# Three unrolled loops rolled up, a TensorE wait moved to the end of its loop, and one prefetch moved behind a loop turn

## The reference

```
for i in range(DEPTH):                       # 4
    mod_x = silu_c @ w_mod[i] + b_mod[i]     # the same for the context
    hx = rms_norm(x, norm_g[i]) * (1 + scale_x) + shift_x
    oc, ox = (_rwkv7_mixer, _na_mixer, _s5_mixer)[i % 3](hc, hx, ...)
    x = x + gate_x * ox
# _rwkv7_step, for 16 heads of 64 channels, in both directions over the tokens:
    sa = einsum(state, kk)
    state = state * w - sa * (kk * a) + v * k
    y = einsum(state, r)
```

## Time and profile before

| | |
|---|---|
| time, median of 3 runs | 6884.97 us (6882.52 to 6889.81) |
| the profiled execution | 6884.97 us, its span 6883.1 us |
| PE busy | 5779.3 us (84%) |
| DVE, ACT, POOL busy | 44%, 29%, 27% |
| granted TensorE clock, mean | 0.920 |
| recurrence of layer 0, from the first window on | 808.8 to 2066 us |
| recurrence of layer 3 | 5461.6 to 6719 us |
| the S5 loop of four turns | 3859 to 4168 us |

### The profile page before, as it was taken

The page is one execution under the profiler, slowest core; times in us unless marked ns, Lnnn a source line. Parts: engine busy times, 40 slices in busy tenths (PEclk is TensorE's granted clock), DMA queues, the critical chain, the costliest instruction groups (busy, mean ns, idle before and its releaser), DMA issues. The chain is left out here.

```text
span 6883.1 us, 212951 instructions
## 1 busy us (share of the span) xinstructions
PE 5779.3 (84%) x91944; PEld 3883.9 (56%) x91944; DVE 3053.5 (44%) x6329; ACT 1984.0 (29%) x3317; POOL 1860.7 (27%) x2006
## 2 busy tenths in 40 slices
PE   5999788888888699978896984396999888888887
PEld 4555577777774355445553553343455577777773
DVE  6200366656661233145514478422300266666662
ACT  1000254444440222134302232111000244544440
POOL 4452244434340336000003540000000144444431
PEclk8999899999998899989898997698999999999998
DMA  3222100110002222132122337422111100011002
GB/s 121 86 99 81 42 30 30 43 37 30 30 30 93 111 98 80 39 95 54 49 82 103 96 94 73 124 70 97 55 69 69 49 30 30 30 43 37 30 30 89
DMA packets 196079, 443.13 MB, mean 64 GB/s; under 512 B 24768, under 2 KB 108608, under 8 KB 195648
## 3 DMA queue, kind: packets, MB, share of 16 engines
q1 hardware_dynamic: 160896, 338.58, 16.4%
q10 hardware_dynamic: 34752, 98.61, 3.6%
HBM read 329.14 MB, written 107.97 MB: 64 GB/s over the span
## 5 line engine op out<-in xcount | busy, mean ns | idle before, releaser
L357 PE MATMUL ps<-arena 128*128 128x512 f32 (+1 forms) x4672 | 1711.0, 528 | 84.9 <-DMA arena<-s_w_in 34.8
L357 PEld LDWEIGHTS ps<-arena 128*128 128x128 f32 x4672 | 886.6, 190 | 903.9 <-issue 864.7
L1861 PE MATMUL ps<-arena 64*64 64x64 f32 x35840 | 736.6, 225 | 161.4 <-ACT arena L2246 59.1
L153 POOL TENSOR_TENSOR arena<-arena 128x512 f32<-128x512 f32 (+1 forms) x360 | 329.0, 930 | 1801.9 <-DMA arena<-w_mod 1791.6
L1861 PEld LDWEIGHTS ps<-arena 64*64 64x64 f32 x35840 | 641.6, 137 | 247.7 <-issue 230.3
L2246 ACT COPY arena<-ps 128x512 f32<-128x512 f32 (+1 forms) x880 | 535.8, 630 | 535.1 <-PE ps L1861 523.1
L2389 POOL TENSOR_TENSOR arena<-arena 128x256 f32<-128x256 f32 (+1 forms) x320 | 299.6, 944 | 895.5 <-DVE arena L2610 456.5
L571 PE MATMUL ps<-arena 128*128 128x512 f32 (+1 forms) x1152 | 423.9, 528 | 41.0 <-DMA arena<-na_w_in 41.0
L1622 DVE SCALAR_TENSOR_TENSOR arena<-arena 128x1280 f32<-128x1280 f32 (+2 forms) x128 | 152.5, 1265 | 617.3 <-PE ps L357 502.7
L2314 POOL MEMSET arena<- 128x1280 f32 (+4 forms) x22 | 15.1, 739 | 1467.9 <-POOLq L83 1467.9
L156 POOL TENSOR_TENSOR arena<-arena 128x256 f32<-128x256 f32 (+2 forms) x504 | 383.1, 772 | 52.0 <-issue 2.1
(11 more groups left out here) (260 smaller groups left out, 9788.6 us busy)
## 6 DMA issues: line engine op xcount, KB each, us to landing
arena<-proj SPq DMA_DIRECT2D x158, 640.0 KB, 5.0
proj<-arena ACTq DMA_DIRECT2D x96, 640.0 KB, 3.9
arena<-w_mod SPq DMA_DIRECT2D x96, 512.0 KB, 7.6
arena<-rw_w SPq DMA_DIRECT2D x68, 512.0 KB, 3.6
arena<-xres SPq DMA_DIRECT2D x40, 640.0 KB, 6.7
xres<-arena ACTq DMA_DIRECT2D x24, 640.0 KB, 6.5
arena<-na_w_in SPq DMA_DIRECT2D x24, 512.0 KB, 3.6
arena<-x SPq DMA_DIRECT2D x16, 640.0 KB, 6.6
```

Of the source, the lines that this page charges most:

```text
L153: self.nc.gpsimd.tensor_tensor(out, strip[:, c:c + n, :], self.k.cond[:, c:c + n, s:s + 1].to_broadcast([P, n, P]), ALU.mult)
L357: last = nc.tensor.matmul(k.ps[:, 3 * u + n, 0:b - a], w[:, c * P:(c + 1) * P], src[:, c, a:b], start=(c == 0), stop=(c == KT - 1))
L1861: last = PE.matmul(part_of(out, dst, hh, g, d), part(l, src, hh, g, d), rhs, start=True, stop=True)
```

## The change

- `NORM_FILL` goes from 19 and 148 to 21 and 147.
- In `s5_prepare`, SP issues the modulation part i+4 after turn i and no more ahead of it. Part 7 stays ahead of turn 3, so the order is turn 0, part 4, turn 1, part 5, turn 2, part 6, part 7, turn 3. PE's program is as before.
- In `rwkv_recur`, PE's two waits and the hold go from the head of the turn to its end, after the last `widened`; they ask for the same events, and the credits of `scale_ev` and `y_ev` go down by 3 and 1 to fit.
- The eight turns of ACT, POOL and DVE become `Fori` loops.

```
-NORM_FILL = {0: 19, 3: 148}
+NORM_FILL = {0: 21, 3: 147}
...
                     if u % 4 == 3 and not last:
                         sp.wait_ge(chunk_mm, i * 6 + (3 + u // 4 * 3))
                         strip(i * 2 + (KT + 2 + u // 4), u // 4)
+                if not last:
+                    hidden.sync_part(sp, i + 4)
 
             with sp.Fori(0, 3) as i:
-                hidden.sync_part(sp, i + 4)
                 turn(i, False)
             hidden.sync_part(sp, 7)
             turn(3, True)
...
-            sem("gate_sig"), sem("gated", 1), sem("scale_ev", 3), sem("post_done"))
+            sem("gate_sig"), sem("gated", 1), sem("scale_ev"), sem("post_done"))
-        y_mm, y_ev = sem("y_mm"), sem("y_ev", 2)
+        y_mm, y_ev = sem("y_mm"), sem("y_ev", 1)
...
             with pe.Fori(0, KT) as e:
-                pe.wait_ge(scale_ev, e * 3 + 3)
-                pe.wait_ge(y_ev, e * (NCH // 4) + 1)
-                hold(k, pe)
                 with pe.Fori(0, NW2) as w:
                     window(e * NW2 + w, e * (NW2 + 1) + w)
...
                 def y_seen(i):
-                    return y_ev, e * (NCH // 4) + (i + 3)
+                    return y_ev, e * (NCH // 4) + (i + 2)
...
                 pe.wait_ge(bonus_ev, e * 3 + 3)
                 widened(SCALE_BANK, 2, wide_post, scale_mm)
+                pe.wait_ge(scale_ev, e * 3 + 3)
+                pe.wait_ge(*y_seen(3))
+                hold(k, pe)
...
-                act.wait_ge(y_ev, e * (NCH // 4) + 2)
+                act.wait_ge(y_ev, e * (NCH // 4) + 1)
...
-            for e in range(KT):
+            with act.Fori(0, KT) as e:
...
-            for e in range(KT):
+            with pool.Fori(0, KT) as e:
...
-            for e in range(KT):
+            with dve.Fori(0, KT) as e:
```

## The result

The changed kernel takes 7007.25 us (median of 4 runs, 7000.49 to 7023.34) against 6887.39 us (median of 4, 6882.52 to 6899.74) of the kernel before: a ratio of 1.0171, 95% interval 1.0154 to 1.0187, or 118 us on 6887 (106 to 129). Forecast were 7048 us, 163 us more, with 7012 as the low end. The sign and the places are as forecast: three new stalls in the S5 loop and a longer gap at each seam of the recurrence. What failed is the sum, above all the term for what comes back in the S5 loop, where 30 us came back for the 10 that I had taken.

What follows compares the result with a forecast made beforehand. PE's program was taken to bound the kernel, so only PE's waits move the end. From the profiled 6885 us: + 120 (S5 loop, net) + 36 (moved wait) + 3 (loops) + 4 (register work) = 7048 us, range 7012 to 7098.

Steps and rivals of the forecast that it cites:

- The direction and the places: Whole kernel slower (0.97); three new S5 waits of 43 to 44 us, about 8 us idle at 14 recurrence seams.
- The stalls: S5 loop, ends of turns 0, 1 and 2: PE waits for POOL's part, 44 + 2 x 43 = 130 us.
- The load leg: S5 loop: loads go out near 3935.5, so POOL begins the part at 3945.5; PE wants it at 3935.89.
- What comes back: S5 loop: 6 us of PE's input waits and 8 us of its DVE waits go, against 4 us clock loss.
- The clock: S5 loop, after each of three pauses: 4.7 us of work at half speed, 4 us added in all.
- The moved wait: Recurrence seams: PE's branch now follows the wait; net 2.6 us, 14 times, 36 us, bounds 14 to 59.
- the code that comes late: Recurrence, behind the seam's branch: second code block may come late; +0.5 us a seam together with a longer low clock.
- The three loops: Recurrence loops of DVE, ACT and POOL: any DVE start fetch is covered by PE's lateness; 0.2 us a seam, 3 us.
- a rival in which DVE becomes the bound: Recurrence seam: DVE's loop misses each turn, +49 us and more in place of 3, about 7094 us; chance 0.08.
- Register work: Recurrence turns: register work for the waits, at places behind a drain; 0.25 us a turn, 16 turns, 4 us.
- The windows' code no longer fits: Recurrence window loop: 64 inner branches must fetch, 3.25 us each, 208 us, or 104 in one layer; chance 0.07.

Runs made afterwards that it cites:

- experiment 7: Kernel before with POOL's weighting of the last four modulation parts replaced by one small addition each; ratio 0.9953, 32 us less.
- experiment 3: Kernel before with PE's wait moved to the turn's end, credits and fills to match, loops of ACT, POOL and DVE unrolled; ratio 1.0035, 24 us more.
- experiment 6: Kernel before, unchanged, measured and profiled again, with the recurrence pieces of all profiles then compared; ratio 0.9996.
- Experiment 11: Kernel before with 60 more filler instructions in front of layer 0's recurrence (79 for 19); ratio 1.0320, 220 us more.

## Right and wrong, step by step

**The direction and the places.** Right: three waits on L180 at L187, the seam's idle at about 8 us, quick inner branches, windows after the first as they were. No rival happened as a whole.

**The stalls** (130 us forecast). Measured 117.4 (123.9 less the 6.5 that the first wait of this kind takes in either): mis-sized by 13. The load leg was right to 0.2 us. The 34.4 us for POOL's part was read where DVE worked beside it; during the stall POOL works alone and takes 30.1.

**What comes back** (10 us forecast). This is the term that failed: 117.4 - 86.9 = 30.5 us came back. I had taken 6 us of the waits for inputs, 8 of those for DVE, and 4 off for the clock, and had limited the return to 20 in my bounds. The runs show 9.0 us for the inputs, 14.0 for DVE (19.3 + 1.6 fell to 5.2 + 1.7), and some 7 us more from the clock instead of a loss. Why DVE gave 14 is in experiment 7: POOL's weighting holds up DVE's operations, and the stall moves it out of the turn. I saw that DVE would run "without POOL working beside it" and gave it no price of its own.

The clock had its sign wrong. PE's busy time over the four turns, by the sums over their stretches (before from 3858.5 to 4165.3 us, after from 3869 to 4266.7, whose stalls have no busy time), falls from 276.8 to 269.9 us for the same work:

```profile
sum 306.80, PE 276.84 PEld 175.78 DVE 203.15 ACT 94.36 POOL 127.09; mean PE 69.21 PEld 43.94 DVE 50.79 ACT 23.59 POOL 31.77
```

```profile
sum 397.70, PE 269.85 PEld 173.26 DVE 154.73 ACT 94.42 POOL 115.91; mean PE 44.98 PEld 28.88 DVE 25.79 ACT 15.74 POOL 19.32
```

The granted clock of one turn of after, from the end of a stall to the start of the next, was

```profile
core 0: us, PE busy (x) PEld busy (x) DVE busy (x) ACT busy (x) POOL busy (x), PEclk, DMA share, GB/s
3977.50:3990.00 12.50, 12.50 (x62) 8.29 (x64) 4.59 (x12) 1.53 (x4) 0.00 (x0) 0.72 0.09 16
3990.00:4016.90 26.90, 26.90 (x211) 17.71 (x208) 13.91 (x37) 11.90 (x27) 0.00 (x0) 1.00 0.31 89
4016.90:4043.80 26.90, 26.88 (x192) 16.79 (x190) 16.16 (x43) 9.58 (x21) 0.00 (x0) 1.00 0.28 70
```

So there is a slow start behind the stall, as forecast, but PE then works at 1.00 until the next one, where before's turns have means of 0.87, 0.89, 0.93 and 0.95. Without the stalls, after's four turns have 0.93, 0.95, 0.93 and 0.90. Why before's turns lie below that is not shown. Together the two terms make the S5 loop 33 us cheaper than forecast.

**The moved wait** (36 us forecast). The seam is right: +3.9 us for +3.5, by the branch that is no longer covered. The sum came out at 35 us by the pieces of experiment 3, but that is luck, and the time says 24 (16 to 32). In the first window the waits on DVE and POOL gave back 1.6 to 2.2 us a turn, for my 1.4. But idle "issue" there grew by about as much, from some 3 to some 5 us (the code that comes late, for which I had 0.5 with the clock), so that PE's idle time in the window is as before. The return of 1.2 to 1.4 us is PE's own work at a higher clock, 0.90 for 0.84, where I had said that the longer pause would keep it low. The rest of the turn, which I had at nothing, gave back about 1 us more (experiment 6).

**The three loops** (3 us). Right, and for the reason given: DVE's start is fetched, at 3.3 us, and PE's late start covers it. By the pieces it is 0.2 to 0.4 us a turn, 3 to 6 us. I had also expected fewer packets on q14; there are 39 for 38. The Trainium skill (Runtime: NRT & Kernel Launch, section Instruction fetch mechanics) has these engines return with a fetch from a body beyond what they hold. I had made that a rival in which DVE becomes the bound; the fetch is there in every turn (the 3.29 us above), the bound is not. Uncovered it costs 2.7 us in the first window and not 3.5.

**Register work** (4 us). 0.27 us a turn in the shortest steps, as forecast (0.25).

**Not in the sum at all.** The share of the steps and of the other windows at the lower clock: between the two profiles the steps fall by 14 x 0.91 = 13 us where the register work adds 4, so that the clock took off 17, and the other windows lost 14 x 0.37 = 5 more. By the thirteen profiles of experiment 6 about 16 us of such a gain go with the longer pauses, and the rest is chance.

**The windows' code no longer fits.** This rival did not happen in after. Experiment 11 shows that the rival's danger is real, at most 60 instructions away, and its price twice the one I gave: 3.25 us for the branch, where 7.1 were lost, since with one more block to reach the loop fetched several in each round.

Balance of the profiled executions: forecast 120 + 36 + 3 + 4 = 163; measured 86.9 (S5) + 21.2 (recurrence) + 4.3 (elsewhere) = 112.4. Of the 51 us between them 33 are the S5 terms and 22 the clock and the windows, and the 4 elsewhere go the other way. By the measured times, which over several runs even out much of the chance, the S5 edit is 83 us for 120, and the rest 28 for 43.

## What to carry to other kernels

In this loop, a load that an engine needs at the end of the turn has its best place neither behind the turn, where its whole chain becomes a stall, nor at the head, where it queues ahead of the turn's own first loads, but inside: late enough that the small loads go first, early enough for the chain to be over. When pricing a stall, ask what it gives back: work that slowed the critical path from beside it is now done while nothing runs, and its duration must be read where it is alone. Read the granted clock over the whole stretch behind a pause, and not only over its first microseconds: here it was low for the first 5 to 12 us and full behind them. When a forecast term comes out right, look whether its parts did. A wait behind a loop's branch hides the branch's fetch, one in front of it does not, and an engine made late by that can hide another's fetch.

## What the chip showed that I had not expected

- DVE and POOL, both on two operands in SBUF, hold each other up: DVE's 128x288 operation takes 451 to 455 ns alone and 448 to 1294 beside POOL's, with the median unchanged at 452. It is some of the operations that wait, not all that run slower. The Trainium skill (SBUF — State Buffer, section Who interferes with whom) describes the pair of ports that the two engines share as an exclusive lock, and not as shared bandwidth; that spread agrees. What it costs a turn is shown by experiment 7 (10.1, 8.1 and 10.0 us, a part of it through the clock), not by the page.
- A loop body shifted by 60 instructions cost 7.1 us a round where the miss of a branch costs 3.5, with 31 packets of code in a turn for 13.
- Kernels with longer pauses of PE had a higher granted clock behind them: 0.978 for 0.967 over the rest of a recurrence turn, and PE's busy time in the S5 loop fell from 276.8 to 269.9 us.
- DVE's loop branch takes 55 to 63 ns by the trace even where its target must be fetched; the fetch shows as 3.3 to 3.5 us of idle time before the next operation. PE's shows in the branch itself (3.5 us) at the outer loop and, in experiment 11, mostly behind it. A short branch is no sign that nothing was fetched.
